# Down-projection weights split by two DMAs of the Pool queue instead of by VectorE

## The reference

```python
D_MODEL = 1024; SEQ = 512; D_FF = 2816; CONV_W = 3
def conv_ffn(h, w_up, conv_w, conv_b, w_down):
    S = h.shape[1]
    u = h @ w_up
    gate, up = u[..., :D_FF], u[..., D_FF:]
    gp = jnp.pad(gate, ((0, 0), (CONV_W - 1, 0), (0, 0)))
    conv = conv_b + conv_w[0] * gp[:, 0:S]
    for i in range(1, CONV_W):
        conv = conv + conv_w[i] * gp[:, i:i + S]
    return (jax.nn.silu(conv) * up) @ w_down
for i in range(DEPTH):
    ...
    x = x + y
    x = x + conv_ffn(rmsnorm(x, ffn_norm[i]), f_w_up[i], f_conv_w[i], f_conv_b[i], f_w_down[i])
return rmsnorm(x, final_norm)
```

## Time and profile before

| what | before |
|---|---|
| time, median of 3 runs (lowest to highest) | 1130.38 us (1130.28 to 1130.58) |
| span of the profiled execution, first to last instruction | 1127.7 us |
| PE busy | 1106.2 us (98%) |
| DVE busy | 578.1 us (51%) |
| ACT busy | 484.9 us (43%) |
| POOL busy | 160.9 us (14%) |
| mean granted TensorE clock | 0.997 of full speed |

### The profile page before, as it was taken

The page is one execution under the profiler, slowest core; times in us unless marked ns, Lnnn a source line. Parts: engine busy times, 40 slices in busy tenths (PEclk is TensorE's granted clock), DMA queues, the critical chain, the costliest instruction groups (busy, mean ns, idle before and its releaser), DMA issues.

```text
span 1127.7 us, 14060 instructions
## 1 busy us (share of the span) xinstructions
PE 1106.2 (98%) x5162; PEld 904.4 (80%) x5162; DVE 578.1 (51%) x734; ACT 484.9 (43%) x707; POOL 160.9 (14%) x123
## 2 busy tenths in 40 slices
PE   6999999999999999999999999999999999999996
PEld 4888778888888888887788888778888888888886
DVE  4588566455555543234354556765555555542214
ACT  6366554445544432222652345454545444431211
POOL 6100021111111110001021221121111111110001
PEclk9999999999999999999999999999999999999998
DMA  6511122322223332221223211222222232333222
GB/s 192 162 65 57 44 100 90 103 93 93 93 97 105 110 103 94 86 95 57 77 84 94 83 43 67 76 95 94 93 93 93 103 102 93 107 103 103 81 73 75
DMA packets 31622, 103.48 MB, mean 92 GB/s; under 512 B 3873, under 2 KB 8641, under 8 KB 31586
## 3 DMA queue, kind: packets, MB, share of 16 engines
q1 hardware_dynamic: 27680, 100.68, 26.8%
q10 hardware_dynamic: 3906, 2.31, 1.1%
HBM read 99.56 MB, written 2.88 MB: 91 GB/s over the span
## 4 chain that ended last, share of the span: by engine, by line
PE 89%; DVE 5%; ACT 3%; DMA 1%; POOL 1%; issue 1%; SPq 0%; DVEq 0%; POOLq 0%
PE PS L308 79%; DVE WL L999 2%; PE PS L355 1%; PE PS L629 1%; PE PS L408 1%; POOL SS L1343 1%; ACT WH L671 1%; PE PS L426 1%; DVE X L1024 1%; ACT SQ L701 1%; PE PS L416 1%; DMA X<-xT 1%; PE PS L540 1%; PE PS L572 0%; PE PS L559 0%
## 5 line engine op out<-in xcount | busy, mean ns | idle before, releaser
L308 PE MATMUL PS<-XH,WH 128*128 128x512 f32 x992 | 393.8, 397 | 9.4 <-DVE XL L1017 9.3
L308 PE MATMUL PS<-XH,WL 128*128 128x512 f32 x992 | 386.9, 390 | 0.0
L308 PE MATMUL PS<-XL,WH 128*128 128x512 f32 x992 | 386.6, 390 | 0.0
L999 DVE TENSOR_TENSOR WL<-WRAW,WH 128x1024 fp32r<-128x1024 f32 (+1 forms) x169 | 229.1, 1356 | 245.3 <-ACT WH L740 72.1
L308 PEld LDWEIGHTS PS<-XH,WH 128*128 128x128 f32 x992 | 186.6, 188 | 52.7 <-issue 11.8
L308 PEld LDWEIGHTS PS<-XL,WH 128*128 128x128 f32 x992 | 186.8, 188 | 39.3 <-issue 1.7
L308 PEld LDWEIGHTS PS<-XH,WL 128*128 128x128 f32 x992 | 186.5, 188 | 39.6
L1353 POOL TENSOR_TENSOR CV<-CV,R 128x512 f32<-128x512 f32 x44 | 70.6, 1604 | 416.8 <-ACT CV L717 416.8
L308 PE MATMUL PS<-AH,WL 128*128 128x512 f32 x308 | 121.4, 394 | 0.0
L308 PE MATMUL PS<-AH,WH 128*128 128x512 f32 x308 | 121.4, 394 | 0.0
L308 PE MATMUL PS<-AL,WH 128*128 128x512 f32 x308 | 121.4, 394 | 0.0
(11 more groups left out here) (204 smaller groups left out, 1206.8 us busy)
## 6 DMA issues: line engine op xcount, KB each, us to landing
WRAW<-w_up SPq DMA_DIRECT2D x88, 512.0 KB, 3.3
WRAW<-w_down SPq DMA_DIRECT2D x32, 704.0 KB, 4.1
WRAW<-w_bin SPq DMA_DIRECT2D x24, 512.0 KB, 3.3
WRAW<-w_qkv SPq DMA_DIRECT2D x11, 512.0 KB, 4.7
WRAW<-w_o SPq DMA_DIRECT2D x7, 512.0 KB, 3.4
WRAW<-w_bo SPq DMA_DIRECT2D x7, 512.0 KB, 3.3
X<-xT SPq DMA_DIRECT2D x4, 512.0 KB, 6.7
out<-X SPq DMA_DIRECT2D x5, 256.0 KB, 2.2
```

The costliest lines, as they stand in the source:

```text
L308: last = mm(PS[:, bank], w[:, c:c + P], x[:, kb], start=start and n == 0 and w is wh and x is hi, stop=stop and n == len(kbs) - 1 and w is wl)
L999: tt(WL[:, s, 0:k * P], WRAW[:, s, 0:k * P], WH[:, s, 0:k * P].bitcast(F32), ALU.subtract)\
```

## The change

SP no longer loads the down weights, and DVE no longer makes their low part. For each down unit, POOL now issues a first DMA from HBM straight into `WH`, which converts float32 to float32r on the way (`load_hi`); ACT writes the negated copy, `WL` = -`WH` (`minus_hi`); and POOL issues a second DMA of the same weights, which adds them onto `WL` (`load_lo`, with `accum_op=ALU.add`). PE waits for that second DMA (`lo_landed`). `load_hi` waits for the slot as SP did; `load_lo` waits for ACT (`hi_ready`). ACT's piece of work for d0+3 has moved behind the last feed-forward step. The weights of all other units go the old way. All counts of semaphores follow (`lo_count`, `raw_count`).

```diff
         @block.tensor
+            def down_lo(layer, j, s):
+                pe.wait_ge(lo_landed[s], 4 * j + (64 * layer + 16 - 4 * s))
+
-            def down_unit(u, s, half):
-                pe.wait_ge(lo_ready, u + 1)
+            def down_unit(u, j, s, half, layer):
+                down_lo(layer, j, s)
                 if half == 0:
                     pe.wait_ge(unit_evac, u - 3)
...
-            pe.wait_ge(lo_ready, DOWN1 + 16)
+            down_lo(1, 14, 2)
+            down_lo(1, 15, 3)
             last_tile(0, range(FT)).then_inc(last_done, 1)
...
         @block.sync
-            load_all(DOWN0, w_down[0], 2 * KT_D, HALF)
...
-            load_all(DOWN1, w_down[1], 2 * KT_D, HALF)
...
         @block.scalar
+            def minus_hi(layer, s, landed):
+                act.wait_ge(hi_landed[s], landed)
+                A(WL[:, s], WH[:, s].bitcast(F32), ACT.Copy, scale=-1.0).then_inc(hi_ready, 1)
...
                 hi_unit(d0 + 2)
-                ffn_step(layer, FT - 1, 1, after=lambda: hi_unit(d0 + 3))
+                ffn_step(layer, FT - 1, 1)
+                hi_unit(d0 + 3)
                 with act.Fori(1, KT_D - 1, 2) as i:
                     for j in range(2):
-                        s, landed = 2 * j, 8 * i + (4 * d0 + 24)
-                        act.wait_ge(raw_landed[s], landed)
-                        nc.scalar.copy(WH[:, s], WRAW[:, s]).then_inc(hi_ready, 1)
+                        s, landed = 2 * j, 8 * i + (64 * layer + 24)
+                        minus_hi(layer, s, landed)
                         act.wait_ge(unit_evac, 2 * i + (d0 + 2 * j))
                         x_tile(st + 1, i + (j - 1), j)
-                        act.wait_ge(raw_landed[s + 1], landed)
-                        nc.scalar.copy(WH[:, s + 1], WRAW[:, s + 1]).then_inc(hi_ready, 1)
+                        minus_hi(layer, s + 1, landed)
...
         @block.vector
-                ffn_step(layer, FT - 2, 0, mid=lambda: lo_unit(d0), after=lambda: lo_unit(d0 + 1))
-                ffn_step(layer, FT - 1, 1, mid=lambda: lo_unit(d0 + 2), after=lambda: lo_unit(d0 + 3))
+                ffn_step(layer, FT - 2, 0)
+                ffn_step(layer, FT - 1, 1)
                 with dve.Fori(1, KT_D - 1, 2) as i:
                     for j in range(2):
-                        s = 2 * j
-                        lo(2 * i + (d0 + 2 * j + 2), s, HALF)
                         x_add(2 * i + (d0 + 2 * j - 1), i + (j - 1), 2 * j, 2)
                         if st + 1 < 4:
                             x_lo(st + 1, i + (j - 1))
-                        lo(2 * i + (d0 + 2 * j + 3), s + 1, HALF)
...
         @block.gpsimd
-                with pool.Fori(0, FT, 2) as i:
+                def gate(f, j):
+                    pool.wait_ge(silu_ready, f + (FT * layer + 1))
+                    nc.gpsimd.tensor_tensor(CV[:, j], CV[:, j], R[:], ALU.mult).then_inc(slr_ready, 1)
+                    pool.wait_ge(slr_ready, f + (FT * layer + 1))
+
+                def load_hi(j):
+                    u, s = DOWN[layer] + j, j % 4
+                    pool.wait_ge(unit_done, u - SLOTS + 1)
+                    pool.dma_start(WH[:, s], w_down[layer, j]).then_inc(hi_landed[s], 16)
+
+                def load_lo(j):
+                    u, s = DOWN[layer] + j, j % 4
+                    pool.wait_ge(hi_ready, u + 1)
+                    pool.dma_start(WL[:, s], w_down[layer, j], accum_op=ALU.add).then_inc(lo_landed[s], 16)
+
+                with pool.Fori(0, FT - 2, 2) as i:
                     for j in range(2):
-                        pool.wait_ge(silu_ready, i + (FT * layer + j + 1))
-                        nc.gpsimd.tensor_tensor(CV[:, j], CV[:, j], R[:], ALU.mult).then_inc(slr_ready, 1)
-                        pool.wait_ge(slr_ready, i + (FT * layer + j + 1))
+                        gate(i + j, j)
+                load_hi(0)
+                load_hi(1)
+                gate(FT - 2, 0)
+                load_lo(0)
+                load_hi(2)
+                gate(FT - 1, 1)
+                load_lo(1)
+                load_hi(3)
+                load_lo(2)
+                load_lo(3)
                 for m in range(KT_D if st + 1 < 4 else KT_D - 1):
+                    if m < KT_D - 2:
+                        load_hi(4 + 2 * m)
+                        load_hi(5 + 2 * m)
+                        load_lo(4 + 2 * m)
+                        load_lo(5 + 2 * m)
                     sum_square(st + 1, m)
```

More of the change, by code:

```diff
@@ L185, in trunk @@
         hi_ready, lo_ready = sem("hi_ready"), sem("lo_ready")
+        hi_landed = [sem(f"hi_landed{s}") for s in range(SLOTS)]
+        lo_landed = [sem(f"lo_landed{s}") for s in range(SLOTS)]
         unit_done = sem("unit_done")
@@ L226, in ksize, with lo_count @@
             return HALF if DOWN0 <= u < B_V or u >= DOWN1 else KT_D
+        def lo_count(u, downs=0):
+            if isinstance(u, int):
+                downs = 16 * ((u >= B_V) + (u >= DOWN1 + 16))
+            return u + (1 - downs)
         @block.sync
@@ L311, in product, with unit @@
                 return last
-            def unit(u, s, hi, lo, bank=None, banks=4, **kw):
-                pe.wait_ge(lo_ready, u + 1)
+            def unit(u, s, hi, lo, bank=None, banks=4, downs=0, **kw):
+                pe.wait_ge(lo_ready, lo_count(u, downs))
                 if not isinstance(u, int) or u >= 4:
@@ L332, in up_phase @@
                     for s in range(SLOTS):
-                        unit(i + (u0 + s), s, XH, XL)
-            def down_unit(u, s, half):
-                pe.wait_ge(lo_ready, u + 1)
+                        unit(i + (u0 + s), s, XH, XL, downs=16 * layer)
+            def down_lo(layer, j, s):
+                pe.wait_ge(lo_landed[s], 4 * j + (64 * layer + 16 - 4 * s))
+            def down_unit(u, j, s, half, layer):
+                down_lo(layer, j, s)
                 if half == 0:
@@ L348, in down_phase @@
                     if s == 1:
-                        pe.wait_ge(lo_ready, u0 + 2)
+                        down_lo(layer, s, s)
                         last = None
@@ L358, in down_phase @@
                     else:
-                        down_unit(u0 + s, s, s % 2).then_inc(unit_done, 1)
+                        down_unit(u0 + s, s, s, s % 2, layer).then_inc(unit_done, 1)
                 with pe.Fori(4, 2 * KT_D - (4 if layer else 0), 4) as i:
                     for s in range(SLOTS):
-                        down_unit(i + (u0 + s), s, s % 2).then_inc(unit_done, 1)
+                        down_unit(i + (u0 + s), i + s, s, s % 2, layer).then_inc(unit_done, 1)
             pe.wait_ge(first_lo, 1)
@@ L447, in _ @@
                     u = A_O + p
-                    pe.wait_ge(lo_ready, u + 1)
+                    pe.wait_ge(lo_ready, lo_count(u))
                     pe.wait_ge(unit_evac, u - 3)
@@ L592, in _ @@
                     head_square(h - 1)
-                pe.wait_ge(lo_ready, u + 2)
+                pe.wait_ge(lo_ready, lo_count(u + 1))
                 pe.wait_ge(unit_evac, u)
@@ L666, in _, with raw_count, hi @@
             A = nc.scalar.activation
-            def hi(u, s, turn, k):
-                act.wait_ge(raw_landed[s], 16 * turn + 16)
+            def raw_count(u):
+                return 16 * (u // 4 + 1) - 64 * (u >= B_V)
+            def minus_hi(layer, s, landed):
+                act.wait_ge(hi_landed[s], landed)
+                A(WL[:, s], WH[:, s].bitcast(F32), ACT.Copy, scale=-1.0).then_inc(hi_ready, 1)
+            def hi(u, s, landed, k):
+                act.wait_ge(raw_landed[s], landed)
                 nc.scalar.copy(WH[:, s, 0:k * P], WRAW[:, s, 0:k * P]).then_inc(hi_ready, 1)
             def hi_unit(u):
-                if u in fifth:
-                    act.wait_ge(raw_landed[0], 16 * (u // 4) + 16)
+                if DOWN0 <= u < B_V or u >= DOWN1:
+                    layer = int(u >= DOWN1)
+                    j = u - DOWN[layer]
+                    minus_hi(layer, j % 4, 16 * (j // 4 + 1) + 64 * layer)
+                elif u in fifth:
+                    act.wait_ge(raw_landed[0], raw_count(u))
                     nc.scalar.copy(fifth[u][1][:], fifth[u][0][:]).then_inc(hi_ready, 1)
                 else:
-                    hi(u, u % 4, u // 4, ksize(u))
+                    hi(u, u % 4, raw_count(u), ksize(u))
             def after_wait(m):
@@ L732, in ffn @@
                     for j in range(2):
-                        s, landed = 2 * j, 8 * i + (4 * u0 + 24)
+                        s, landed = 2 * j, 8 * i + (4 * u0 + 24 - 64 * layer)
                         act.wait_ge(raw_landed[s], landed)
```

4 lines of the change are left out of this document (2 added, 2 removed).

## The result

The changed kernel takes 1154.9 us (median of 4 runs, 1152.55 to 1156.75) against 1130.33 before: 1.0219 times as long, 95% interval 1.0206 to 1.0233, 24.6 us slower. The forecast was 1164 us, 33.6 us slower, in a range of 1145 to 1270. The profiled execution spans 1153.5 us, 25.8 more than that of before. In the runs that have both figures the device time lies 1.7 to 1.9 us above the span; so some 0.9 of the 2.7 us between span and median before, which the forecast added, were not around the instructions but the difference between that execution and the median. That is also why spans differ by 25.8 us and medians by 24.6.

The account below looks back on a forecast made before the run. PE was taken to bound the kernel, so DVE's relief gives 0. Turn waits of 28.2 us, 2.4 at the last tile and 2.8 of slow clock made 33.4, giving 1164 us, 3.0% slower, range 1145 to 1270.

Parts of the forecast that it names:

- What bounds the kernel: Whole kernel: PE sets the time nearly 1 to 1; removing 52.0 us of DVE subtractions gives 0.
- The sum: Whole kernel: 28.2 us turn waits, 2.4 last tile and 2.8 slow clock add 33.4 us, giving 1164 us.
- the case of the sum: Whole kernel: 1153 to 1185 us, with POOL issue of 0.33 to 2.2 us, adding DMA up to 5 us; chance 0.47.
- rival 2: Down-weight DMAs: adding costs no more than a plain load, 2.2 us of engine time; 1144 to 1153 us, chance 0.10.
- The walk through the turn: From up to down phase: low parts queue behind POOL's gates; PE waits 5.6 and 8.5 us, 14.1 per layer.
- the landing: Down-weight DMAs, from POOL taking one until it lands: 5.1 us for a converting, 7.3 for an adding one.
- both pages' prices: Skill-page estimates at the turn: 3.7 us converting, 5.3 adding; some 20 us in all instead of 33.
- The loop of pairs: Down units after the turn: DMAs hold engines 13.2 of 15.4 us per pair; no PE wait except the last tile.
- Rival 1: Down phases: DMA engines or slow POOL issues become the bound; chance 0.25 up to 1270 us, 0.13 above.
- The last tile of layer 1: End of layer 1's down phase: PE wants units 14 and 15 together, after 15.4 us, and waits 2.4 us.
- The clock: After long PE waits, matmuls run slow: 1.4 us charged per layer on the second down unit, 2.8 for both.
- Not slower: At the turn: low parts land soon enough for PE; 1130 to 1133 us; chance 0.05 including anything overlooked there.

## Why the prediction was right

**What bounds the kernel.** Right. PE sets the time, and relieving DVE gives 0: 1129.5 us with the subtractions gone.

**The sum.** In the traces, by the forecast's terms: 21.0 us for the two turns up to PE's start on d0+1 (10.2 and 10.8) where it had 28.2, 4.4 us of slow matmuls on d0+1 where it had 2.8, and no wait at the last tile where it had 2.4: 25.3 instead of 33.4. So the terms did not miss the same way, and the errors cancelled in part. The time, 1154.9, lies at the low edge of the case of the sum (1153 to 1185), 2 us above what rival 2 reached (1144 to 1153); the time alone would hardly tell the two apart, the engine time of the adding DMA does.

**The walk through the turn.** Its mechanism was right at every step, and its sizes were nearly all a little too large. Low part of d0: issued 400.4, landed 407.7 predicted; 399.6 and 406.0 measured. High part of d0+2: 409.9 against 407.6. Gate of FT-1 over: 416.6 against 413.4. Low part of d0+1: 423.9 against 419.8. PE's waits: 5.6 and 8.5 predicted, 3.8 to 4.1 and 3.8 to 4.3 measured. The second is 4.2 us shorter because the low part of d0+1 lands 4.1 us sooner. The end of d0 came out as forecast, 415.4, by two errors that cancel: PE starts on it 1.6 us sooner, and it takes 9.3 us instead of 7.7, since its matmuls are slow for a while.

The term that was mis-sized is the landing. I put 7.3 us for a lone adding DMA and 5.1 for a converting one, of which the issue was 1.3. They took 6.1 to 6.5 and 4.2 to 4.3. POOL's instruction lasts 0.9 us for an adding and 0.55 for a converting DMA, so the middle between SP's issue and POOL's longest instruction was too high; the engine time of 4.4 us for the adding was close to the 4.1 measured. The gates took 1.28 us and not the 2.0 that I kept for them, nor the 2.20 of before; the run without the subtractions shows the same 1.29 in the kernel before. This is the one relief of DVE that did reach the path, 0.9 us per gate against before.

The pages of the Trainium skill named in the prediction can now be judged. The Trainium skill's "Collectives: The Full Stack" (the bandwidth ceiling) states the half rate of a ReduceScatter against an AllGather, and explains it by the two source reads of each piece; the adding DMA here comes near it, 4.1 against 2.2 us, a factor of 1.9, though no run shows that the second read is the cause. The fixed 2.0 us plus bytes of the Trainium skill's "DMA: Bandwidth & Descriptors" (the anatomy of one DMA) gives an estimate of 3.7 us for a converting copy of this size, and 4.2 to 4.3 were measured. The walk with both pages' prices gave about 20 us in all; measured were 24.6, the prediction's sum gave 33.4, so the pages' prices came nearer, with both a little too low where the prediction's were too high.

**The loop of pairs.** Right: no wait, at a share of 0.82 to 0.84 in both layers (450 to 511.6 and 1040 to 1090 us) where 0.86 was forecast. Rival 1 was not reached. It needs little more: one transfer more per unit makes PE wait in the loop, and a PE that is quicker by 3% waits there for 1.1 us.

**The last tile of layer 1.** Wrong: 2.4 us forecast, none measured. The last low part is issued at 1116.6 and lands 8.1 us later; PE comes to the last tile at 1125.65, 1.0 us after that. The walk had put that issue later, behind dearer ones. The margin is thin all the same: with the waits filled PE waits there for 0.5 us, and with one more transfer per unit for 5.2.

**The clock.** Right in kind, and a bit small: 1.4 us after a long wait forecast, 1.8 and 2.5 measured for d0+1, and 3.7 us in all given back by filling the waits.

**The rivals.** Adding at the price of a copy would have given 1147 to 1153; the run without adding took 1145.1 us, 2 us below that. "Not slower" did not come about by quick landings, as no row had allowed. It does come about by another order in POOL's queue, which the prediction did not consider as it was no part of the change.

## What to carry to other kernels

When a transfer moves to an engine that also computes, look first at what stands ahead of it in that engine's queue, not at its bandwidth: here 24 us hung on where two adding DMAs stood in the queue (one more DMA moved with them), while 23 MB of additional traffic cost nothing. An adding DMA of 704 KB held the DMA engines for 4.1 us, a copy for 2.2, and a copy issued right behind it landed after 7.5 us instead of 4.3; keep what another engine waits for ahead of it. And when an experiment adds a tile, put it where it moves nothing, or run the tile alone: the six microseconds of a displaced region looked like a gain from the edit.

## What was not expected of the hardware

- A matmul's spacing depends on where its operands lie, the data in one case, the weights (`GA`) in the other: 33 matmuls took 7.70, 7.48, 7.55, 7.70 and 7.70 us with the region of `AH` and `AL` moved by 0, 64, 128, 192 and 256 bytes. The 16 matmuls on `GA` took 3.73 us unmoved, 3.62 with 64 bytes and 3.73 again with 128.
- The price of a wait in slow matmuls is not set by its length. In layer 0, after waits of 3.8 and 4.3 us, the first three matmuls still begin 0.23 to 0.34 us apart before the 0.43 us spacing comes, and d0+1 takes 9.51 us; in layer 1, after 4.1 and 3.8 us, they are slow almost from the first, and d0+1 takes 10.24. In the run with only the low part of d0 ahead both waits were 6.2 us, and d0+1 took 10.72 and 9.59 us.
- DMAs that convert float32 to float32r, issued by POOL, land 4.2 to 4.3 us after their issue when nothing is ahead of them, against a median of 4.1 for plain ones of the same size by SP, and hold the DMA engines as long, 2.2 us.
- Work on DVE lengthens work on POOL beside it: a gate of 128x512 takes 2.20 us in the kernel before and 1.29 where DVE's subtraction of 128x1408 is gone.
